# Differential attention: first two input tiles by turns, the residual's second half through VectorE and device memory, the first two turned blocks in one visit

## What is computed

```python
h = h + swiglu(rms_norm(h, norm_ffn[i]), ffn_w_in[i], ffn_w_out[i])
gate = jax.nn.sigmoid(rms_norm(h, ple_norm[i]) @ ple_w_gate[i])
h = h + gate * (p[i] @ ple_w_proj[i])          # layer 0 ends here
...
hn = rms_norm(h, norm_mix[1])                  # layer 1: differential attention
q, k, v = split(hn @ diff_w_in)                # 1024 x 3072
q, k = rope(rms_norm(q, g_q)), rope(rms_norm(k, g_k))     # per head of 64
a = softmax(q1 k1) - lam * softmax(q2 k2)      # 8 heads, each a pair of scores
y = rms_norm(a @ v, g_sub) * (1 - lambda_init) @ diff_w_out
```

## Time and profile before

| | us |
|---|---|
| median of 3 runs | 900.74 (900.65 to 902.83) |
| the profiled execution | 900.89 |
| its span in the profile | 898.7 |

### The profile page before, as it was taken

One profiled execution on the slowest core, in us unless ns is written; L12 is line 12 of the kernel. 1 busy time (PEld: TensorE's weight loads), 2 busy tenths in 40 slices (PEclk: granted clock), 3 DMA queues, 4 the chain that ended last, 5 costly groups with the idle time before them and its releaser, 6 DMA issues.

```text
span 898.7 us, 12238 instructions
## 1 busy us (share of the span) xinstructions
PE 892.9 (99%) x4364; PEld 737.0 (82%) x4364; DVE 654.6 (73%) x997; ACT 506.1 (56%) x820; POOL 63.4 (7%) x75
## 2 busy tenths in 40 slices
PE   9999999999999999999999999999999999999998
PEld 8988888888888888778888888888888888887777
DVE  6985478777735699997787776646679897779764
ACT  6756555444444667688564444435664544587681
POOL 0001000000000003211100000000010000215100
PEclk9999999999999999999999999999999999999999
DMA  7674458766755655424487667746568775656621
GB/s 271 197 240 143 162 189 301 277 242 243 240 194 194 227 199 201 160 97 141 139 284 265 237 239 246 254 142 231 202 220 278 260 253 192 207 200 234 227 70 47
DMA packets 76988, 187.47 MB, mean 209 GB/s; under 512 B 6852, under 2 KB 31812, under 8 KB 76936
## 3 DMA queue, kind: packets, MB, share of 16 engines
q1 hardware_dynamic: 75480, 182.99, 59.6%
q0 software_dynamic: 1024, 3.15, 1.0%
q10 hardware_dynamic: 432, 0.66, 0.2%
HBM read 171.83 MB, written 14.94 MB: 208 GB/s over the span
## 4 chain that ended last, share of the span: by engine, by line
PE 95%; DMA 2%; issue 2%; DVE 1%; POOL 1%; ACT 0%; DVEq 0%; POOLq 0%
PE bank L1801 84%; PE bank L1839 3%; PE bank L1854 1%; PE bank L2114 1%; PE bank L2140 1%; DMA mb_pT<-mb_blocks 1%; DMA mb_blocks<-p_tok 1%; DMA h<-x_dram 0%; PE bank L2224 0%; PE bank L2125 0%; PE bank L2253 0%; PE bank L1961 0%; PE bank L2009 0%; PE bank L2013 0%; PE bank L2100 0%
## 5 line engine op out<-in xcount | busy, mean ns | idle before, releaser
L671 ACT ACTIVATE whi<-raw 128x1024 fp32r<-128x1024 f32 x295 | 306.2, 1060 | 186.3 <-DMA raw<-stream_dram 108.8
L1079 DVE TENSOR_TENSOR wlo<-raw,whi 128x1024 fp32r<-128x1024 f32 x295 | 347.5, 1213 | 55.6 <-ACT whi L671 54.8
L1801 PE MATMUL bank<-whi,x_hi 128*128 128x512 f32 x560 | 152.5, 394 | 0.0
L1801 PE MATMUL bank<-wlo,x_hi 128*128 128x512 f32 x560 | 149.9, 389 | 0.0
L1801 PE MATMUL bank<-whi,x_lo 128*128 128x512 f32 x560 | 149.8, 389 | 0.0
L1801 PEld LDWEIGHTS bank<-wlo,x_hi 128*128 128x128 f32 x560 | 105.1, 188 | 22.3
L1801 PEld LDWEIGHTS bank<-whi,x_lo 128*128 128x128 f32 x560 | 105.1, 188 | 22.0
L1801 PEld LDWEIGHTS bank<-whi,x_hi 128*128 128x128 f32 x560 | 103.4, 188 | 21.7 <-issue 1.2
L1801 PE MATMUL bank<-whi,y_hi 128*128 128x512 f32 x396 | 108.0, 394 | 0.1
L1801 PE MATMUL bank<-wlo,y_hi 128*128 128x512 f32 x396 | 106.0, 390 | 0.0
L1801 PE MATMUL bank<-whi,y_lo 128*128 128x512 f32 x396 | 106.0, 389 | 0.0
(11 more groups left out here) (251 smaller groups left out, 891.4 us busy)
## 6 DMA issues: line engine op xcount, KB each, us to landing
raw<-stream_dram SPq DMA_DIRECT2D x295, 512.0 KB, 4.6
ffn_blocks<-ffn_blk SPq DMA_DIRECT2D x22, 256.0 KB, 2.0
ffn_land<-ffn_blocks SPq DMA_DIRECT2D x22, 256.0 KB, 3.7
second_blocks<-h_blk SPq DMA_DIRECT2D x8, 256.0 KB, 2.0
h_land<-second_blocks SPq DMA_DIRECT2D x8, 256.0 KB, 3.1
cv_blocks<-cv_blk SPq DMA_DIRECT2D x7, 256.0 KB, 5.2
cv_land<-cv_blocks SPq DMA_DIRECT2D x7, 256.0 KB, 3.3
h_blocks<-h_blk SPq DMA_DIRECT2D x3, 512.0 KB, 6.3
```

What stands on the lines that cost most here:

```text
L671: A(whi[:, u % RING, :], raw[:, u % RAW, :], ACT.Copy).then_inc(sem("w_hi"), 1)
L1079: V.tensor_tensor(wlo[:, u % RING, :], raw[:, u % RAW, :], whi[:, u % RING, :].bitcast(F32), ALU.subtract).then_inc(sem("w_lo"), 1)
L1801: last = T.matmul(bank[pair + t][:, :], lhs[a][:, kt, t * P:(t + 1) * P], w[:, u % RING, kk * NW:(kk + 1) * NW], start=part != 1 and k == ...
```

## The change

`DF_IN` joins `PAIRED`: its first two tiles are taken by turns, and the second half of h goes through DVE's blocks and device memory. The step `("second", 0)` goes away with its 8 transposes; `lhs_hi` and `lhs_lo` for banks 6 and 7 are replaced by `second_hi` and `second_lo`. Since tile 0 now ends at unit 6 instead of 4, the table moves: ACT's `tile 0` from 4 to 6, DVE's `rope 0` from 5 to 7, `more 0` from 6 to 8 (behind `sums 0`), PE's `qkT 0` from 8 to 11, where it stands right ahead of `qkT 1`, and ACT's copies of both to 11. `use(name)` only numbers the uses of the shared semaphores.

```diff
-PAIRED = (FFN_IN0, FFN_IN1, CV_IN, MB_IN)
+PAIRED = (FFN_IN0, DF_IN, FFN_IN1, CV_IN, MB_IN)
+USES = ("mix0", "gate0", "df", "mix1", "gate1", "cv", "mb")
...
 DF_ORDER = {
     "pe": (
-        (1, "second", 0), (8, "qkT", 0), (11, "qkT", 1), (12, "qkT", 2), (13, "scores", 0), (13, "qkT", 3),
+        (11, "qkT", 0), (11, "qkT", 1), (12, "qkT", 2), (13, "scores", 0), (13, "qkT", 3),
...
     "act": (
-        (4, "tile", 0), (8, "tile", 1), (9, "qkT", 0), (12, "qkT", 1), (12, "tile", 2), (12, "qkT", 2),
+        (6, "tile", 0), (8, "tile", 1), (11, "qkT", 0), (11, "qkT", 1), (12, "tile", 2), (12, "qkT", 2),
...
     "dve": (
-        (5, "rope", 0), (6, "more", 0), (6, "sums", 0), (8, "rope", 1), (8, "sums", 1), (10, "more", 1),
+        (7, "rope", 0), (7, "sums", 0), (8, "more", 0), (8, "rope", 1), (8, "sums", 1), (10, "more", 1),
...
                 done = gate_blocks(n, tin + FT + 2)
-            done = second_blocks(4, CV_IN)
+                if n == 0:
+                    done = second_blocks(use("df"), DF_IN)
+            done = second_blocks(use("cv"), CV_IN)
...
                 split_to(END[tple + 4] + 1 + AHEAD)
-                if n == 0:
-                    lhs_hi(Y, norm_gain(j + 1), (6, 7))
                 squares(j + 1, 1)
-                if n == 1:
-                    second_hi(j + 1, X, 4, END[CV_IN] - 1)
+                second_hi(j + 1, X if n else Y, use("cv" if n else "df"), END[tple + 4] - 1)
...
-                    elif n == 0:
-                        split_to(END[DF_IN] + 1 + AHEAD)
-                        lhs_lo(dst, norm_gain(j + 1), (6, 7))
                     else:
                         second_blk(12 * n + 10)
-                        second_lo(j + 1, dst, 4, END[CV_IN] - 1)
+                        second_lo(j + 1, dst, use("cv" if n else "df"), END[tple + 4] - 1)
...
-            product(DF_IN, Y, "df_in", need=df_half0, beside=df_beside)
-            for t in range(1, 6):
+            first_tiles(DF_IN, Y, "df_in", list(half) + second_need(use("df")), df_beside)
+            for t in range(2, 6):
                 product(DF_IN + t, Y, "df_in", beside=df_beside)
```

More of the change, by code:

```diff
@@ L492, in second_blocks @@
             def second_blocks(r, tile):
-                at = END[tile] + (7 if tile == CV_IN else 8)
+                at = END[tile] + (7 if tile in (DF_IN, CV_IN) else 8)
                 fetch(done, at)
@@ L528, in _ @@
                 done = END[out_tile]
-                done = second_blocks(2 * n, tin)
+                done = second_blocks(use(f"mix{n}"), tin)
                 fetch(done, done_at(tin) + 10)
@@ L550, in _ @@
             done = max(done, END[MB_IN])
-            done = second_blocks(5, MB_IN)
+            done = second_blocks(use("mb"), MB_IN)
             fetch(done, UNITS)
@@ L694, in mixer_lhs @@
                 squares(j, 1)
-                second_hi(j, dst, 2 * (j - 1) // 3, END[out + 4])
+                second_hi(j, dst, use(f"mix{(j - 1) // 3}"), END[out + 4])
             def second_hi(j, dst, r, base):
@@ L729, in next_lhs @@
                 squares(j, 1)
-                second_hi(j, dst, 5, END[first + 1])
+                second_hi(j, dst, use("mb"), END[first + 1])
             def evacuate(tile, j, dst, width, signal, func=ACT.Copy, scale=None):
@@ L873, in ffn @@
                         for k in range(TT):
-                            act.wait_ge(sem(f"g_land{k}"), 16 * (2 * n + 2))
+                            act.wait_ge(sem(f"g_land{k}"), 16 * (use(f"gate{n}") + 1))
                             for kt in range(4):
@@ L1146, in parts_out @@
                 second_blk(4 * (j - 1) + 2)
-                second_lo(j, dst, 2 * (j - 1) // 3, END[out + 4])
+                second_lo(j, dst, use(f"mix{(j - 1) // 3}"), END[out + 4])
             V.memset(warm[:, :], 0.0).then_inc(sem("warm"), 1)
@@ L1411, in ffn @@
                             for kt in range(4):
[L1412 removed]
+                                dve.wait_ge(sem("g_hi"), 4 * use(f"gate{n}") + 2 * k + kt // 2 + 1)
                                 at = slice(k * P, (k + 1) * P)
@@ L2053, in ffn @@
                 other = Y if src is X else X
-                first_tiles(tin, src, "ffn_mid", list(got) + second_need(2 * n))
+                first_tiles(tin, src, "ffn_mid", list(got) + second_need(use(f"mix{n}")))
                 product(tin + 2, src, "ffn_mid")
@@ L2080, in ffn @@
                 product(tple + 1, PT, "ple_gated", need=[("pT", 2 * (n + 1))])
-                half1 = []
+                half1, r = [], use(f"gate{n}")
                 product(tple + 2, src, "ple_sig")
-                half1 += [("g_lhs", 2 * (2 * n + 1) + k + 1, ("g_hi", 4 * (2 * n + 1) + k + 3)) for k in range(2)]
+                half1 += [("g_lhs", 2 * r + k + 1, ("g_hi", 4 * r + k + 3)) for k in range(2)]
                 product(tple + 3, PT, "ple_gated")
@@ L2143, in df_av @@
                 last.then_inc(sem("df_av"), 1)
-            df_half0, df_pairs = list(half) + [None, None], [None] * 4
+            df_pairs = [None] * 4
             def df_beside(u):
@@ L2150, in df_beside @@
                         continue
-                    if step == "second":
-                        df_half0[2:4] = h_T(1, 3)
-                    elif step == "qkT":
+                    if step == "qkT":
                         df_T(arg)
@@ L2180, in cv_T @@
                 free[b] = ("cv_lhs", 8)
-            first_tiles(CV_IN, X, "cv_prod", list(half) + second_need(4))
+            first_tiles(CV_IN, X, "cv_prod", list(half) + second_need(use("cv")))
             product(CV_IN + 2, X, "cv_prod")
@@ L2288, in mb_beside @@
                         mb_zT(arg)
-            first_tiles(MB_IN, X, "mb_in", list(got) + second_need(5), mb_beside)
+            first_tiles(MB_IN, X, "mb_in", list(got) + second_need(use("mb")), mb_beside)
             for t in range(2, 8):
```

8 lines of the change are left out of this document (5 added, 3 removed).

## The result

| | before | after |
|---|---|---|
| median, us | 901.01 (899.6 to 903.98, 8 runs) | 906.87 (905.14 to 908.89, 8 runs) |
| the profiled execution | 900.89 | 907.48 |
| its span | 898.7 | 905.7 |

The change made the kernel slower, by a factor of 1.0062, with an interval of 1.0051 to 1.0074.

The account below looks back on a forecast made before the run. PE, busy 892.9 of 898.7 us, bounds the kernel, with DVE close behind in `DF_IN`. Terms -1.1 + 4.7 + 3.2 - 0.28 = 6.5, taken as 6.6 from `qkT 2`'s start: 900.74 + 6.6 = 907.3 us, range 904.4 to 909.3.

Parts of the forecast that it names:

- Nothing was expected back behind `qkT 2`: Behind `qkT 2` all engines keep their old order, so the 6.6 us of delay there stays to the end.
- No wait at unit 4: In `DF_IN`, first high parts are ready at 337.07, unit 4 begins at 338.63: round trip hidden by 1.6 us.
- The first new wait: PE waits ahead of unit 8 for ACT's tile 0, queued behind unit 12's high part: +4.7 us, until 354.3.
- The second at `qkT 2`: PE comes to `qkT 2` at 366.2 and waits for DVE's rescaling of tile 1 until 369.4: +3.2 us.
- DVE has no room there: Between unit 1 and unit 12 DVE has 0.1 us to spare; what it does later delays `qkT 2`.
- the central case: Both new waits and the saving as summed, clock at full: 905.8 to 908.6 us; chance 73%.
- a granted clock below full behind 354: Sign of being wrong: PE's clock not fully granted after 354 us, where the wait ahead of unit 8 ends.
- DVE's lateness: DVE's last operation on the left factor in `DF_IN` ends at 339.94 instead of 336.47: 3.47 us late.
- Unit 12's transfer: From the end of `wlo` 8 to ACT's high part of unit 12: 4.83 us, the disputed size.
- this rival: PE's clock falls in a wait: 1.7 us lost, swallowed after unit 8's wait, 909.0 after `qkT 2`'s; chance 8%.
- The saving: PE in `DF_IN`: 0.95 us for the transposes and slower unit behind, 0.13 for one visit; together -1.1 us.
- the single visit: `qkT 0` and `qkT 1` in one PE visit save one slower unit: 0.13 us.

Follow-up runs that it names:

- e1: The changed kernel with only ACT's step for tile 0 moved back from table position 6 to 4: 908.12 us, factor 1.0085 on the kernel before.
- e5: The changed kernel with only ACT's step for tile 0 moved from table position 6 to 5: 909.59 us, factor 1.0084 on the kernel before.
- e2: e1 with DVE's rope 0, more 0 and sums 0 back at 5, 6 and 6: 905.63 us, factor 1.0055 on the kernel before.
- e0_after: The changed kernel again, unedited, on another chip: 908.48 us, factor 1.0078 on the kernel before.
- e3: e2 with rotation factors and lambda's products computed early, in the gated embedding, and lambda's exponential moved ahead: 905.07 us, factor 1.0054 on the kernel before.
- e6: The changed kernel with h's second half turned by PE again, no trip through device memory, order kept: 905.72 us, factor 1.0050 on the kernel before.
- e10: e3 with DVE's more 1 and unit 1 at 9 instead of 10, one low part moved behind them: 903.97 us, factor 1.0037 on the kernel before.
- e8: The kernel before with only qkT 0 and ACT's copy of it moved to 11, beside qkT 1: 900.86 us, factor 1.0002.
- e9_tile2: e3 with DVE's tile 1 steps ahead of two low parts, and ACT's tile 2 and qkT 2 at 11: 904.49 us, factor 1.0030 on the kernel before.

## Why the prediction was right, point by point

**The time.** 907.3 was forecast, 6.6 above the kernel before. Measured were 906.87, and factors that make +5.6 and +7.0 us of 901. Nothing was expected back behind `qkT 2`; in the profiled executions the distance of 7.35 there is 7.0 in the spans, so nearly nothing came back.

**The mechanism** was right in its waits and in what ends them, and left out the clock. No wait at unit 4. The first new wait ahead of unit 8, for the copy of tile 0 that stands behind unit 12's high part. The second at `qkT 2`, behind DVE. That DVE has no room there was shown by e1 and e5 (a wait taken from PE ahead of unit 8 came back) and by e2 (2.2 us of DVE's order gave 2.5).

**The clock** is where the central case was wrong. The central case, with 73% of the chances, had it at full throughout, and the prediction named "a granted clock below full behind 354" as a sign of being wrong. It was 0.55 in unit 8, from 354.97 to 359.85. The number stands all the same, since the 2.16 us lost lie ahead of a wait that was to be 3.2 us.

**DVE's lateness** was predicted as 3.47 us. In the profiled execution of the change it was more: the last `y_lo` ended at 339.57 + 1.14 = 340.71 instead of 339.94, since DVE waited 1.55 us for ACT's second copy and not 0.74, and ACT for the landing. That 0.77 runs through all that follows: unit 12's high part at 351.50 (350.75 predicted), `rope 0` at 354.32 (353.6), `unit 1`'s end at 370.05 (369.3), `qkT 2` at 370.16 (369.4). But it is no error of the sum. In e0_after, the same kernel, the row is

```profile
338.85 1.14 DVE L1138 SCALAR_TENSOR_TENSOR y_lo<-h_land,cols,y_hi 128x128 fp32r<-128x128 f32 x4 [0.66 <-ACT y_hi L712]
```

and it ends 9.57 us after the block transposes began (330.42), where 9.67 was predicted.

**Unit 12's transfer** was priced well: from the end of `wlo` 8 (344.56 + 2.27 = 346.83) to ACT's high part 4.67 us, 4.83 predicted. The landings of `raw` from 335 to 352 us took 3.3 at least, 5.0 in the median and 6.9 at most:

```profile
DMA to landing us min/median/max: 3.3/5.0/6.9
```

The estimate of 3.2 by the Trainium skill ("DMA: Bandwidth & Descriptors", "Anatomy of one DMA") holds for the shortest only, as the prediction had weighed it. That section gives its figures for transfers that GpSimd issues; these were issued by SP.

**The two waits** were 5.49 and 1.07 where 4.7 and 3.2 were predicted. The first is longer by the 0.75 of DVE. The second is shorter since PE came there at 369.09 and not 366.2: 0.75 for the longer first wait and 2.16 for the half clock behind it, while DVE's end moved by 0.75 alone. The prediction had named this rival and what it would cost ("swallowed"), but only for a small share of the chances. The Trainium skill's rule ("TensorE: Matmul & The Clock Gate", "HAM oscillation"), that a long gap of PE brings the half rate, agrees with the trace here (0.55 granted in unit 8, behind the wait of 5.49 us). By it the prediction had put the loss behind the second wait, 909.0; a loss there stood only in the kernels where the wait at `qkT 2` was the long one (e1, e2, e3, e5, e6, e10).

**The saving** of 1.1 us was real, and drowned: with PE waiting, transposes taken from PE save nothing. e8 shows that the 0.13 of the single visit was too small to be seen.

What stays open: what makes the second half of the blocks land up to 1.3 us earlier or later from one execution to the next. No run here shows it. And no kernel was found that has the new order and beats the one before; the best, e10_unit9 and e9_tile2, are 0.3 to 0.4% behind it.

## What to carry to other kernels

Before taking work from the busiest engine, look at the place where it comes in: an engine that is busy for 17.79 of 18.10 us right there is as much a bound as the one with 99%, though its share of the whole is 73%. Follow a chain through it to the next meeting point, since the delay there is the cost, however it is shared out among waits. And in a stream where a buffer's release starts the next fetch, putting a step ahead of a release defers a transfer that some other engine will wait for, with its own queue behind it.

## What the runs showed of the hardware

TensorE's clock is lost in waits of a few microseconds, inside a kernel in which PE is busy for 99% of the span. Behind every wait of 3.16 us or more in `DF_IN` (3.16, 3.51, 3.83, 4.73, 4.88, 5.18, 5.22, 5.25 and 5.49) matmuls ran at half the rate, a group of four of 128x512 in up to 2.06 us instead of 1.17. Where it was worked out, 1.6 us were lost behind waits of 3.16, 3.51 and 3.83 us, 2.0 to 2.25 behind 4.88, 5.22, 5.25 and 5.49, and 2.9 behind 4.73, so the longest wait did not cost the most. Behind waits of 2.13, 1.65 and 1.39 us a group took 1.16 to 1.18, which is the full clock; between 2.13 and 3.16 nothing was measured. So the wait of 3.16 us cost some 4.7 in all. Where another wait follows, the loss disappears in it.

Of four fetches of 512 KB that went out within 2 us of each other (e3_early) the last three came 1.2 to 1.3 us apart, by the starts of ACT's high parts at 341.62, 342.89 and 344.12. That is slower than ACT takes them (3.89 for four). So a fetch that is held up for a few us isn't caught up by issuing several at once.
